# Two tiles moved by 32 bytes, three by 128, in the partitions of SBUF

## What is computed

```
u = jnp.square(jax.nn.relu(h @ mlp_w1[i])) @ mlp_w2[i]          # twice, 1024 -> 4096 -> 1024
...
(jax.nn.silu(x @ w_gate) * (x @ w_up)) @ w_down                 # four times, 1024 -> 2816 -> 1024
...
h = h + jax.nn.sigmoid(h @ ple_gate_w[i]) * (p[i] @ ple_w[i])   # twice, after the first kind
```

## Time and profile before

| | us |
|---|---|
| median of 3 runs | 3253.31 (3252.62 to 3253.32) |
| the profiled execution | 3254.09 |
| its span, first to last instruction | 3252.4 |
| PE busy within the span | 3209.2 |

### The profile page before, as it was taken

One profiled execution on the slowest core, in us unless ns is written; L12 is line 12 of the kernel. 1 busy time (PEld: TensorE's weight loads), 2 busy tenths in 40 slices (PEclk: granted clock), 3 DMA queues, 4 the chain that ended last, 5 costly groups with the idle time before them and its releaser, 6 DMA issues.

```text
span 3252.4 us, 47396 instructions
## 1 busy us (share of the span) xinstructions
PE 3209.2 (99%) x20092; PEld 2855.6 (88%) x20092; DVE 2032.9 (63%) x2889; ACT 1416.7 (44%) x2128; POOL 836.4 (26%) x377
## 2 busy tenths in 40 slices
PE   9999999999999999999999999999999999999998
PEld 7887899988778999889998889999899998889997
DVE  6577755445857444486676637667667566466756
ACT  4354544443635444354443324444445333244533
POOL 1210033320500333202322430232123223312322
PEclk9999999999999999999999999999999999999999
DMA  5211223321203232313322322332323223222322
GB/s 174 82 40 55 95 98 117 104 97 62 76 27 110 100 115 100 115 65 105 130 78 91 117 91 71 107 127 79 104 98 119 89 91 117 78 91 98 124 85 78
DMA packets 223219, 308.95 MB, mean 95 GB/s; under 512 B 7872, under 2 KB 151248, under 8 KB 222752
## 3 DMA queue, kind: packets, MB, share of 16 engines
q1 hardware_dynamic: 219424, 291.41, 26.9%
q0 software_dynamic: 3584, 14.52, 1.3%
HBM read 303.80 MB, written 2.10 MB: 94 GB/s over the span
## 4 chain that ended last, share of the span: by engine, by line
PE 70%; DVE 19%; ACT 6%; issue 3%; DMA 1%; POOL 0%; DVEq 0%; SPq 0%; ACTq 0%
PE bank L603 21%; PE bank L605 21%; PE bank L604 21%; DVE wlo L2135 5%; ACT whi L1343 4%; DVE wraw L2157 2%; DVE raw_w L2157 2%; DVE ul_w L2345 1%; PE bank L1001 1%; PE bank L623 1%; DVE zt L2340 1%; DMA wraw<-in_e_w_in 1%; DVE t_w L2340 1%; DVE zt L2196 1%; PE bank L1284 1%
## 5 line engine op out<-in xcount | busy, mean ns | idle before, releaser
L3220 POOL TENSOR_TENSOR wlo<-wraw,whi 128x1024 fp32r<-128x1024 f32 (+1 forms) x189 | 492.5, 2609 | 1318.4 <-ACT whi L1343 1318.3
L603 PE MATMUL bank<-xh,whi 128*128 128x256 f32 (+1 forms) x2456 | 718.2, 292 | 12.3 <-DVE xl L2437 7.9
L605 PE MATMUL bank<-xh,wlo 128*128 128x256 f32 (+1 forms) x2456 | 714.0, 291 | 0.0
L1343 ACT ACTIVATE whi<-wraw 128x1024 fp32r<-128x1024 f32 (+2 forms) x399 | 434.9, 1095 | 633.2 <-PE bank L605 485.5
L604 PE MATMUL bank<-xl,whi 128*128 128x256 f32 (+1 forms) x2456 | 709.8, 289 | 0.0
L3220 POOL TENSOR_TENSOR wlo<-raw_w,whi 128x1024 fp32r<-128x1024 f32 x114 | 291.9, 2564 | 844.9 <-ACT whi L1343 844.9
L603 PEld LDWEIGHTS bank<-xh,whi 128*128 128x128 f32 x2456 | 462.3, 188 | 31.8 <-DVE wlo L2135 11.6
L2135 DVE TENSOR_TENSOR wlo<-wraw,whi 128x1024 fp32r<-128x1024 f32 (+1 forms) x210 | 277.7, 1325 | 317.1 <-ACT whi L1343 316.3
L603 PE MATMUL bank<-whi,uh_w 128*128 128x512 f32 x1216 | 474.4, 390 | 0.6 <-DVE ul_w L2766 0.6
L605 PE MATMUL bank<-whi,ul_w 128*128 128x512 f32 x1216 | 473.4, 389 | 0.0
L604 PE MATMUL bank<-wlo,uh_w 128*128 128x512 f32 x1216 | 473.3, 389 | 0.0
(11 more groups left out here) (402 smaller groups left out, 4970.7 us busy)
## 6 DMA issues: line engine op xcount, KB each, us to landing
wraw<-in_w_in SPq DMA_DIRECT2D x26, 1024.0 KB, 5.0
wraw<-in_ffn_w_gate SPq DMA_DIRECT2D x40, 512.0 KB, 4.3
raw_w<-in_ffn_w_gate SPq DMA_DIRECT2D x40, 512.0 KB, 4.8
raw_w<-in_ffn_w_up SPq DMA_DIRECT2D x40, 512.0 KB, 4.2
wraw<-in_ffn_w_up SPq DMA_DIRECT2D x40, 512.0 KB, 4.3
wraw<-in_ffn_w_down SPq DMA_DIRECT2D x20, 1024.0 KB, 5.0
raw_w<-in_ffn_w_down SPq DMA_DIRECT2D x20, 1024.0 KB, 5.0
raw_w<-in_mlp_w SPq DMA_DIRECT2D x19, 1024.0 KB, 5.0
```

The costliest lines, as they stand in the source:

```text
L603: M.matmul(o, lh, rh, start=start, stop=False, skip_group_check=more)
L605: return M.matmul(o, ll, rh, start=False, stop=stop, skip_group_check=more)
L1343: A.activation(hi, raw, ACT.Copy).then_inc(*k.w_hi.inc(("hi", j)))
L3220: G.tensor_tensor(lo[:, 0:n], raw[:, 0:n], hi[:, 0:n].bitcast(F), ALU.subtract).then_inc(*k.w_lo.inc(("lo", j)))
```

## The change

Two small tiles that nothing reads or writes are allocated ahead of `ah` and behind `al`:

```
             s.raw = [tmp("raw2", [128, SLOT]), tmp("raw3", [128, SLOT])]
+            tmp("a_edge", [128, 8])
             s.ah, s.al = tmp("ah", [128, 3, 4, 256], R), tmp("al", [128, 3, 4, 256], R)
+            tmp("u_edge", [128, 24])
             with nc.sbuf_tensor("u32_w", [128, 2, 8, T], F) as u32:
                 free = [u32[:, 0, :, :], u32[:, 1, :, :]]
             s.uh, s.ul = tmp("uh", [128, 8, T], R), tmp("ul", [128, 8, T], R)
```

## The result

The changed kernel takes 3265.47 us (median of 6, 3264.59 to 3266.53), the kernel before beside it 3253.32 us (median of 6). The ratio is 1.0037, 95% interval 1.0026 to 1.0047: slower by 12.2 us, where 14.3 us less were forecast and the range ended at 3250.

A forecast was written before the change was run, and what follows sets the result against it. TensorE, busy 3209.2 of 3252.4 us, was taken as the bound, its rate set by start addresses. Units -18.3, waits +3.4, `ph` and `pl` +0.6 gave -14.3 us: 3253.3 to 3239.0, range 3234 to 3250.

The forecast's parts named there:

- The units: Cycles of seven products with `ah` or `xh` moving: 19.95 to 19.60 us each, 18.3 us won in all.
- only `ah` gains: Rival on the unit products: `xh` products keep 118.0 ns, so 5.0 us won, 3248.3 us; chance 0.15.
- the low bits do nothing: Rival on the unit products: the SBUF region sets the rate, time 3253.3, at most 0.6 more; chance 0.11.
- I take 0: Down matmuls and small tiles moved by 128: no effect, within bounds of 0 and 23.7 us slower.
- the last rival: Down product needs agreement by 256: 226.8 to 233.3 ns a matmul, +23.7 us, time 3262.6; chance 0.09.
- together 3.4 us: TensorE waits take back 1.8 and 0.6 us at first units, 1.0 in front of product 4 at group ends.
- The bound of one unit's gain: Each of six waits in front of product 4 at group ends swallows between nothing and 0.35 us.
- The 87% busy: DVE's busy share in gated units once a cycle is 1.8% shorter, taken to show the cover holds elsewhere.
- `ph` and `pl`: Product with `ah` stationary, 96 matmuls of 512 columns: 6.5 ns slower each, 0.6 us lost.
- The rival that came true: Down product loses its rhythm as `uh` and `ul` disagree with the weights by 256: +23.7 us, 3262.6; chance 0.09.

The follow-up runs named there:

- e1: Kernel before with `ah` and `al` 32 bytes up, `uh`, `ul`, `t2` and the small tiles 512 up; 3245.58 us, ratio 0.9975.
- e3: Kernel before with `ah` and `al` 64 bytes up, `uh` and `ul` 256 up; 3240.3 us.
- e8: Addresses of e1, weight remainders of product 3 made by DVE in place of POOL; 3246.82 us, ratio 0.9978 to the kernel before.
- e10: Kernel before with `xh` and `xl` 160 bytes up, all behind them 256 up, `ah` and `uh` otherwise as in e3; 3240.25 us, ratio 0.9961.
- e12: As e10, but `ah` and `al` too 64 bytes behind the weights; 3238.34 us, ratio 0.9953 to the kernel before.
- e6: Kernel before with `ah` and `al` 192 bytes up, `uh` and `ul` 288 up; 3261.9 us.

## Why the prediction was wrong

**The units: right.** The forecast was that with the low bits of `xh`, `ah` runs at 116.7 ns, and that `xh` too goes back to its own 116.7 once no product disturbs it. Both came true in the steady part of a group, 19.60 us a cycle. The reading of two rates for the same instruction, by what stands ahead of it, carried this. One part of that reading was too simple: a wait does not always put the fast rhythm back, as the three products at 117.8 ns behind a wait in the changed kernel show. The rival "only `ah` gains" is out, and so is "the low bits do nothing". Outside of waits the two groups lost 16.8 us; 18.3 were forecast.

**`uh` and `ul`, "I take 0": this step failed.** The text gave two bounds, 0 and 23.7 us, and took 0 because slices that are multiples of 512 bytes apart run alike. That is no argument for a step of 128, as the text itself said further down under the last rival. The price of that bound was near: 20.5 us measured, against 23.7. Moves of `uh` by 256 and 512 cost nothing, e1 and e3 show, and every other distance tried costs 2 to 6.5 ns a matmul. The mistake was one of weight: with no row for the aligned pair at another distance, and with `xh` against the weights at 6.5 ns worse in the same form, a chance of 0.09 was too small, and the range should have reached to that bound. On this side stood up to 6.5 ns on each of 3648 matmuls, on the other 2.1 ns (0.35 us over 168) on each of 9072 in the units, so the side without rows could outweigh the side with rows.

**Waits, "together 3.4 us": undersized.** They took 8.1 us. The places in front of product 4 are eight, not six, and each grew by 0.7 us (from 3.20 to 3.90 us for product 3 with the wait behind it), twice the 0.35 that the text allowed. That is 5.8 us where 1.0 was forecast; the other waits took 2.3, near their 2.4. The bound of one unit's gain was wrong: over the last two units and more of such a group DVE goes at its own pace. Two of its instructions before, then the first of them after (the second is the one at 1585.82 under e8):

```profile
1543.56 0.69 DVE L2340 TENSOR_TENSOR t_w<-t_w,bank 128x512 f32<-128x512 f32 x1
...
1580.01 3.42 DVE L2157 TENSOR_TENSOR wraw<-wraw,raw_w 128x1024 f32<-128x1024 f32 x1
```

```profile
1549.46 0.69 DVE L2342 TENSOR_TENSOR t_w<-t_w,bank 128x512 f32<-128x512 f32 x1
```

DVE takes 36.45 us before and 36.36 after, while TensorE, from the start of product 7 beside the first of them to the wait, takes 0.81 us less (45.77, then 44.96). The gain of more than two units so arrives at that one wait. The 87% busy that the text worked with hid a DVE that is late at one place.

**`ph` and `pl`: right in rate, small in effect.** 227 to 233 ns, but half of it came out of a wait; +0.2 in place of +0.6 us.

**The rival that came true** was priced at 3262.6; with the waits as measured it is 3253.3 - 16.8 + 8.1 + 20.5 + 0.2 + 0.4 = 3265.7, against 3265.5. The rules of the Trainium skill that were weighed ("SBUF — State Buffer", section "Specifications (TRN2)": lines of 16 bytes; "TensorE: Matmul & The Clock Gate", section "Step-by-step: what each phase is for": independent read ports) would have left the time alone. The measurements decide against a reading of them in which start addresses do not matter.

## What to carry to other kernels

Where TensorE is the bound and every matmul brings its own weight load, the start addresses of the operands are a setting. In these runs 512 moving float32 columns were fastest with both at the same remainder by 256 bytes. With 256 columns the moving one was best 32 ahead or 64 to either side, where history can take the gain back (117.8 in place of 113 to 117 ns). So try several and read the result from the distances of starts. When one tile is moved, hold all tiles behind it at their old remainder by 256 at least (pad by 256 or 512), or they will pay for it unseen. And price the side that no row covers by the number of instructions on it before putting a chance to it.

## What the runs showed of the hardware

The time between starts of this kernel's matmuls with 128 stationary columns changes with the start addresses, and follows the distance of the two operands by 256 bytes (with the weights at one remainder throughout): 113.3 to 120.0 ns with 256 moving columns, 226.8 to 233.3 ns with 512. The dependence differs between the two sizes: distance 0 has the slowest mean seen for 256 columns (119.8) and the best for 512 (226.8). With 256 columns two steady rates occur for the same instructions and addresses: 113.3 and 117.8 ns at -64 (e10, e12), 116.7 and 117.8 ns at +32 (before, e6). A stream can keep its rate over changes of slice and of unit, and may leave it behind a wait or another product. At +32, 116.7 ns hold over whole groups in the changed kernel; 117.8 to 118.0 ns are seen behind products at distance 0, but also behind a wait with none of them near, and in e3 three products in a row go at 119.9 (2013.20 to 2021.83 us). A DVE subtraction of 128 x 1024 takes 3.42 us where it starts within a POOL subtraction, and 1.21 us in e8 where that POOL instruction is gone.
